# RWKV mixer output computed channel-major from centred values, in a two-layer decoder kernel on one Trainium2 core

## The chip, the cores and the metric

One core of one Trainium2 chip runs the whole program. The metric is the device time of one execution in microseconds (us); the kernel before takes 2488.39 us, the median of three runs. Engine names: PE is TensorE (matmul), PEld its weight load, DVE is VectorE, ACT is ScalarE, POOL is GpSimd, SP is SyncE, which here only issues DMAs.

## The reference, cut to what matters

The program is a decoder trunk of two layers over 256 tokens with model width 2048, in float32. Layer 0 (even) projects the normed input once, and feeds two mixers: differential attention with 8 heads and an RWKV-7 time mix with 16 heads of 64. Layer 1 (odd) is an HGRN2 recurrence. A SwiGLU feed-forward follows each. The change is in the RWKV mixer's output. Of it the reference says:

```python
def step(state, inp):
    rt, wt, kt, vt, kkt, at = inp
    sa = jnp.einsum('bhvk,bhk->bhv', state, -kkt)
    state = state * wt[:, :, None, :] + sa[..., None] * (kkt * at)[:, :, None, :] + vt[..., None] * kt[:, :, None, :]
    return state, jnp.einsum('bhvk,bhk->bhv', state, rt)
...
mean = jnp.mean(y, axis=-1, keepdims=True)
var = jnp.mean(jnp.square(y - mean), axis=-1, keepdims=True)
yn = ((y - mean) * lax.rsqrt(var + RW_GN_EPS)).reshape(B, S, RW_WIDTH) * ln_w + ln_b
bonus = (jnp.sum(r_h * k_h * r_k, axis=-1, keepdims=True) * v_h).reshape(B, S, RW_WIDTH)
return ((yn + bonus) * g).astype(p.dtype)
```

The state, and so y, is linear in the values v. Values from which each head's mean over its 64 channels has been taken give a y that has mean zero in each head.

## The kernel before, in words

Everything is kept channel-major: 128 channels on the partitions, 256 tokens along the free axis. A weight block of 128 output columns is 16 tiles of 128x128. Each block is read from memory by SP, turned into a rounded part on ACT (`Block.high`, line 318) and a remainder on DVE (`Block.low`, line 323), each in two halves of 8 tiles, and multiplied on PE: the rounded part against both parts of the activations (line 333, 512 columns), the remainder against one (line 368, 256 columns). Two converted blocks are resident and two accumulators, `acc`, alternate, so a conversion waits until the block two places before it has been multiplied, and a block's first product waits until DVE has emptied the accumulator (`evacuate`, line 446; in the last step `residual`, lines 1138 and 1140).

The even layer's mixers run in 8 steps, `even_step(j)`, one for each pair of RWKV heads and one attention head. The order in each engine is written out by hand in that function, once for each engine. PE works through the 96 tiles of the next step's six projection blocks, `dense(n)` being the next n tiles, and between them does the small products of the mixers of step j. ACT and DVE put the conversions `high(0..)` and `low(0..)`, numbered by half block, between their mixer work. Each engine runs its own list strictly in the written order. Engines signal through counting semaphores, `S["rw_..."]`. In the last step (`more=False`) the dense tiles are those of the output projection, with all but the two last-made of its 16 input rows.

Two chunks of 128 tokens make an RWKV step. `Vn` are the values turned to token-major, `Us` the solved corrections, `KTR` and `LTR` masked products, `S0` the state between the chunks, `AR` the decayed queries. The output y is token-major in bank 2: for chunk 0 four products with 64 columns (lines 1869 and 1870), for chunk 1 one of 128 (1886) and four of 64 (1889, 1890). The last of them signals `rw_y`. What follows it in the kernel before:

- PE: gate (1894), bonus sums (1896, 1897, signal `rw_bonus`), the 10 dense tiles left, the two transposes of the normalised output (1902, in the trace under the helper's line 1695), which wait for `rw_yn`; then the next step's `rw_za` (1739, 1740), the transposes of its values, the sums of key squares (1747, 1748), 22 dense tiles, and the products `rw_m1` (1757), which wait for `rw_bt`, among others.
- DVE: mean (1364, 1366), subtraction (1368), bonus times value (1372), variance (1374), next values (1151), product with the inverse deviation (1380, `rw_yn`), `evacuate(4)`, `low(13)`, `swap`, `low(14)`; then the next step's scans (1203), and from them a chain to `bk` (1236, `rw_bt`).
- ACT: `key_squares(j + 1)` (737, 738), square of the centred output (855), logarithm (857), exponential (859), a table load, `high(14)`, scale and offset (865), gate copy (867); then the next step's sigmoids (746, 747).

`key_squares` begins with `act.wait_ge(S["rw_bonus"], j)`, called with the next step's number, so with this step's bonus sums: their input `parts` is what it writes over.

Of the kernel before, what the change touches and what calls it, by code (L numbers as in the profile page):

```python
# [13 lines left out]
P = 128  # L14
# [27 lines left out]
C_END = C_QUART + P  # L42
# [4 lines left out]
G_ATT0, G_FFN0, G_ATT1, G_FFN1, G_FIN = 0, 16, 32, 48, 64  # L47
G_LB0, G_LB1 = 80, 96
G_SUB, G_HGN, G_MUW, G_MUG = 112, 113, 114, 115
G_LAM = 116  # L50
# [3 lines left out]
def shape_constants():  # L54
# [18 lines left out]
    c[:, C_QUART:C_QUART + P] = s // 32 == t // 32  # L73
    c[:, C_TRI:C_TRI + P] = s < t
# [15 lines left out]
def build(nc, xT, w_even, w_even_out, w_odd, w_odd_out, w_gu, w_down, w_last, gain_last, consts, gains, par, par_ln, wa_up, g_up, out):  # L90
    with ExitStack() as ctx:
        def sb(name, shape, dt=F32):
            return ctx.enter_context(nc.sbuf_tensor(name, shape, dt))
# [16 lines left out]
        small = sb("small", [P, 96])  # L110
# [17 lines left out]
        def flat(ap):  # L128
            return ap.rearrange("p a b -> p (a b)")
# [32 lines left out]
        yc = take(4, 64)  # L162
        ysq = take(4, 64)
# [80 lines left out]
        ymean = small[:, 20:24]  # L244
        yvar = small[:, 24:28]
        yrs = small[:, 32:36]
# [5 lines left out]
        ars = small[:, 56:58]  # L252
        nrt = small[:, 28:30]
        upper = small[:, 48:52]
        lower = small[:, 92:96]
        hlb = small[:, 60:76]
        homl = small[:, 76:92]
# [4 lines left out]
        def bank(b, n=1):  # L262
            return pm[:, b * 512:(b + n) * 512]
# [9 lines left out]
        for group in (  # L273
# [8 lines left out]
            "rw_S rw_S0 rw_R1 rw_nR1 rw_U1 rw_Us1 rw_y rw_ymean rw_yc rw_ysq rw_yvar rw_yrs rw_yn rw_yT rw_yTs",  # L282
# [383 lines left out]
        def _(act):  # L666
# [73 lines left out]
            def even_step(j, block, more=True):  # L740

                def high(half):
                    block(half // 2).high(act, half % 2)
# [102 lines left out]
                act.activation(Us[:, 0], bank(5)[:, 384:512], ACT.Copy).then_inc(S["rw_Us0"], 1)  # L846
                act.wait_ge(S["rw_R1"], j + 1)
# [3 lines left out]
                high(13)  # L851
                if more:
                    key_squares(j + 1)
                act.wait_ge(S["rw_yc"], j + 1)
                act.activation(ysq, yc, ACT.Square).then_inc(S["rw_ysq"], 1)
                act.wait_ge(S["rw_yvar"], j + 1)
                act.activation(yrs, yvar, ACT.Ln, scale=1.0 / 64, bias=c_gn).then_inc(S["rw_yrs"], 1)
# [4 lines left out]
                act.wait_ge(S["rw_yT"], j + 1)  # L862
                act.wait_ge(S["rw_late"], 32 * j + 32)
                act.wait_ge(S["rw_end"], j + 1)
                act.activation(yT, bank(1)[:, 256:512], ACT.Identity, scale=pln[:, 0:1], bias=pln[:, 1:2]).then_inc(S["rw_yTs"], 1)
# [189 lines left out]
        def _(dve):  # L1055
# [128 lines left out]
            def even_step(j, block, more=True):  # L1184
                def low(half):
                    block(half // 2).low(dve, half % 2)
# [175 lines left out]
                dve.wait_ge(S["rw_y"], j + 1)  # L1362
                y4 = bank(2)[:, 256:512].rearrange("p (a b) -> p a b", a=4)
                dve.reduce_sum(ymean, y4, AX.X).then_inc(S["rw_ymean"], 1)
                dve.wait_ge(S["rw_ymean"], 2 * j + 1)
                dve.tensor_scalar(ymean, ymean, 1.0 / 64, None, ALU.mult).then_inc(S["rw_ymean"], 1)
                dve.wait_ge(S["rw_ymean"], 2 * j + 2)
                dve.tensor_tensor(yc, y4, ymean.unsqueeze(2).broadcast_to([P, 4, 64]), ALU.subtract).then_inc(S["rw_yc"], 1)
# [4 lines left out]
                dve.wait_ge(S["rw_ysq"], j + 1)  # L1373
                dve.reduce_sum(yvar, ysq, AX.X).then_inc(S["rw_yvar"], 1)
# [4 lines left out]
                dve.wait_ge(S["rw_yc"], j + 1)  # L1379
# [302 lines left out]
        def _(pe):  # L1682
# [29 lines left out]
            def even_step(j, block, more=True):  # L1712
# [173 lines left out]
                pe.matmul(bank(2)[:, 384:512], AR[:, 1, 1], S0, start=True, stop=False, skip_group_check=True)  # L1886
                for h in range(2):
                    o, v = bank(2)[:, 384 + 64 * h:448 + 64 * h], slice(64 * h, 64 * h + 64)
                    pe.matmul(o, KTR[:, 2 * h + 1, P:2 * P], Vn[:, 1, v], start=False, stop=False, skip_group_check=True)
                    last = pe.matmul(o, LTR[:, 2 * h + 1, P:2 * P], Us[:, 1, v], start=False, stop=True, skip_group_check=True)  # L1890
                last.then_inc(S["rw_y"], 1)

# [259 lines left out]
```

## Time and profile before

| | |
|---|---|
| time, median of 3 runs (lowest to highest) | 2488.39 us (2487.61 to 2488.83) |
| profiled execution: its own time | 2488.57 us |
| profiled execution: span of the core | 2486.7 us, granted clock 0.999 |
| PE busy | 2468.1 us, 99% |
| DVE, ACT, POOL busy | 1828.9 us (74%), 1236.0 us (50%), 497.9 us (20%) |
| DMA | 438.32 MB, mean 176 GB/s |

The profile is one execution, followed instruction by instruction. Its span is 1.9 us shorter than its own time, which holds some work around the span. A matmul in float32 shows as two records, one in the rounded format or a transpose as one. Ends of matmuls are modelled and overlap the next; the distance between starts is what PE spends. "Idle before" is the time in which an engine had nothing running ahead of an instruction, and behind the arrow stands what ended it.

### The profile page before, as it was taken

What the parts mean: (1) busy time and instruction counts of PE and PEld (TensorE: products, weight loads), DVE (VectorE), ACT (ScalarE), POOL (GpSimd) and SP (SyncE); (2) the same over time, 40 slices, a digit from 0 to 9 for tenths busy, and PEclk for the clock granted to TensorE, in tenths of its full rate; (3) what the DMA queues carried; (4) which work ended last, traced back from release to release, by engine and by line L of the source; (5) the groups of instructions that cost most, each with busy time, mean ns of one, the idle gap of its engine ahead of it and who ended that gap; (6) DMA issues with size and microseconds to landing.
All of it is one profiled execution on the core that took longest, in us unless ns stands there. A gap on an engine that the chain in (4) does not pass through costs nothing.

```text
span 2486.7 us, 45860 instructions
## 1 busy us (share of the span) xinstructions
PE 2468.1 (99%) x16576; PEld 2161.8 (87%) x16576; DVE 1828.9 (74%) x3028; ACT 1236.0 (50%) x1798; POOL 497.9 (20%) x436
## 2 busy tenths in 40 slices
PE   9999999999999999999999999999999999999998
PEld 8888888888888888888888888888888888888887
DVE  7888888766655666566989999997666557655665
ACT  5666666644433443344665656655444434443444
POOL 0123222222200221022222211213222012200220
PEclk9999999999999999999999999999999999999999
DMA  7333233455555555554554445445455555555553
GB/s 273 121 138 133 110 131 120 177 181 192 186 189 192 185 194 186 188 190 173 193 186 169 169 158 179 152 158 216 176 194 186 201 188 186 186 202 185 188 194 127
DMA packets 65570, 438.32 MB, mean 176 GB/s; under 512 B 9408, under 2 KB 10816, under 8 KB 15808
## 3 DMA queue, kind: packets, MB, share of 16 engines
q1 hardware_dynamic: 61632, 436.29, 49.4%
q8 instruction: 64, 1.05, 0.2%
q10 hardware_dynamic: 3840, 0.70, 0.1%
q14 instruction: 34, 0.28, 0.0%
HBM read 434.87 MB, written 2.10 MB: 176 GB/s over the span
## 4 chain that ended last, share of the span: by engine, by line
PE 85%; DVE 8%; issue 4%; ACT 2%; DMA 1%; ACTq 0%; SPq 0%; DVEq 0%
PE acc L333 29%; PE acc L403 17%; PE mixer_banks L414 10%; PE acc L385 9%; PE acc L397 9%; PE acc L368 6%; DVE w_low L323 2%; DVE arena L1568 2%; DVE arena L446 1%; DVE arena L1556 1%; PE mixer_banks L1695 1%; PE acc L330 1%; DVE arena L1558 1%; DMA w_raw<-w_even 1%; PE mixer_banks L1783 0%
## 5 line engine op out<-in xcount | busy, mean ns | idle before, releaser
L318 ACT ACTIVATE w_high<-w_raw 128x1024 fp32r<-128x1024 f32 x831 | 862.9, 1057 | 888.0 <-PE acc L385 387.5
L323 DVE TENSOR_TENSOR w_low<-w_raw,w_high 128x1024 fp32r<-128x1024 f32 x832 | 1047.9, 1286 | 115.3 <-ACT w_high L318 114.4
L333 PE MATMUL acc<-h_split,w_high 128*128 128x512 f32 x3184 | 818.5, 396 | 1.0
L333 PEld LDWEIGHTS acc<-h_split,w_high 128*128 128x128 f32 x3184 | 575.1, 188 | 110.4 <-DVE arena L446 3.1
L565 POOL TENSOR_TENSOR arena<-arena,norm_scale 128x256 f32<-128x256 f32 x152 | 231.3, 1522 | 1348.5 <-DVE arena L446 1328.8
L446 DVE TENSOR_REDUCE arena<-acc 128x256 f32<-128x512 f32 x285 | 196.1, 688 | 289.4 <-PE acc L403 178.2
L403 PE MATMUL acc<-h_split,w_high 128*128 128x512 f32 x1376 | 328.2, 391 | 0.0
L403 PEld LDWEIGHTS acc<-h_split,w_high 128*128 128x128 f32 x1376 | 252.9, 188 | 48.9
L368 PEld LDWEIGHTS acc<-h_split,w_low 128*128 128x128 f32 x1824 | 263.7, 190 | 27.5
L368 PE MATMUL acc<-h_split,w_low 128*128 128x256 f32 x1824 | 273.2, 282 | 0.0
L333 PE MATMUL acc<-mix_split,w_high 128*128 128x512 f32 x752 | 185.6, 392 | 0.6 <-DVE x_residual L1140 0.6
L385 PEld LDWEIGHTS acc<-h_split,w_low 128*128 128x128 f32 x1376 | 176.4, 191 | 6.7
L397 PE MATMUL acc<-h_split,w_low 128*128 128x256 f32 x1376 | 179.1, 283 | 0.0
L385 PE MATMUL acc<-h_split,w_low 128*128 128x256 f32 x1376 | 178.5, 283 | 0.0
L414 PE MATMUL mixer_banks<-w_high,mix_split 128*128 128x512 f32 x704 | 173.9, 389 | 0.0
L397 PEld LDWEIGHTS acc<-h_split,w_low 128*128 128x128 f32 x1376 | 171.3, 192 | 0.0
L333 PEld LDWEIGHTS acc<-mix_split,w_high 128*128 128x128 f32 x752 | 138.1, 188 | 28.1 <-issue 1.3
L414 PEld LDWEIGHTS mixer_banks<-w_high,mix_split 128*128 128x128 f32 x704 | 132.1, 188 | 27.5
L638 POOL TENSOR_TENSOR arena<-arena,norm_scale 128x256 f32<-128x256 f32 x88 | 100.5, 1141 | 47.2 <-ACT arena L943 47.2
L403 PE MATMUL acc<-mix_split,w_high 128*128 128x512 f32 x448 | 107.2, 391 | 0.0
L1138 DVE TENSOR_TENSOR x_residual<-x_residual,acc 128x256 f32 (+1 forms) x80 | 33.5, 419 | 99.2 <-PE acc L403 47.5
L943 ACT ACTIVATE arena<-arena 128x256 f32<-128x256 f32 x88 | 36.9, 419 | 119.5 <-POOL arena L565 119.5
(335 smaller groups left out, 2300.5 us busy)
## 6 DMA issues: line engine op xcount, KB each, us to landing
w_raw<-w_gu SPq DMA_DIRECT2D x176, 1024.0 KB, 4.8
w_raw<-w_odd SPq DMA_DIRECT2D x64, 1024.0 KB, 4.8
w_raw<-w_even SPq DMA_DIRECT2D x49, 1024.0 KB, 4.8
w_raw<-w_last SPq DMA_DIRECT2D x44, 1024.0 KB, 4.8
w_raw<-w_down SPq DMA_DIRECT2D x32, 1024.0 KB, 4.9
w_raw<-w_down SPq DMA_DIRECT2D x16, 768.0 KB, 4.2
w_raw<-w_odd_out SPq DMA_DIRECT2D x12, 1024.0 KB, 4.8
w_raw<-w_even_out SPq DMA_DIRECT2D x10, 1024.0 KB, 4.7
```

Of the source, the lines that this page charges most:

```text
L318: act.activation(wh[:, self.res, ks], raw[:, self.raw, ks], ACT.Copy).then_inc(high_done, 1)
L323: dve.tensor_tensor(wl[:, self.res, ks], raw[:, self.raw, ks], wh[:, self.res, ks].bitcast(F32), ALU.subtract).then_inc(low_done, 1)
L333: pe.matmul(acc[self.acc][:, 0:2 * T], wh[:, self.res, k], flat(both), start=k == 0, stop=stop)
L368: last = pe.matmul(acc[self.acc][:, 0:T], wl[:, self.res, k], split[:, src(k), 0], start=False, stop=k == self.kt - 1, skip_group_check=True)
L385: last = pe.matmul(acc[self.acc][:, 0:T], wl[:, self.res, k], split[:, k, 0], start=False, stop=k == self.kt - 1, skip_group_check=True)
L397: pe.matmul(acc[self.acc][:, 0:T], wl[:, self.res, k], split[:, k, 0], start=k == 0, stop=False, skip_group_check=True)
L403: last = pe.matmul(acc[self.acc][:, 0:2 * T], wh[:, self.res, k], flat(split[:, k]), start=False, stop=k == self.kt - 1, skip_group_check= ...
L414: return pe.matmul(banks[th], split[:, 4 * q + k, c, th * P:(th + 1) * P], flat(w[:, self.res, 4 * k:4 * k + 4]), start=q == 0 and k == 0 ...
L446: dve.reduce_sum(dst, acc[self.acc].rearrange("p (s t) -> p t s", s=2), AX.X).then_inc(evac_done, 1)
L565: pool.tensor_tensor(dst, dst, nrs, ALU.mult).then_inc(S[done], 1)
L638: pool.tensor_tensor(sil[:, b], sil[:, b], nrs, ALU.mult).then_inc(S["hid_scaled"], 1)
L1568: dve.tensor_tensor(*part, ALU.mult).then_inc(S["hg_X"], 1)
```

## The change

In the even steps only:

- The values' transposes become products with a matrix that turns and centres at once: identity less 1/64 within each head. It is a new constant of 128x128, loaded with the others.
- The products for y take their operands the other way round, so that y comes out channel-major: the stationary operand is a head's 64 columns of `Vn` or `Us`, the moving one 128 columns of `KTR` or `LTR`, and the result goes to 64 of the 128 partitions, one head to each half. The mean and its subtraction go away, and so do the two transposes at the step's end.
- The variance is a float32 product of the head ones with the squared output (scaled by 1/8 before the square), in bank 3, and thus there for every channel; the logarithm and exponential are taken of 128x256 in place of 128x4. PE waits for the square ahead of it.
- Four of the ten remaining dense tiles are taken ahead of the gate and bonus products; the variance product stands behind the bonus sums, ahead of the other six.
- `high(13)` on ACT moves ahead of the copies `nR1` and `Us1`; `low(13)` on DVE moves from behind `evacuate(4)` to ahead of the bonus product.
- PE waits for the previous step's `rw_yn` ahead of the sums of key squares, since these write to the bank in which y lies.
- Some small tiles are placed elsewhere, and 16 unused gain columns are left out.

```diff
@@ ACT, even_step
                 act.wait_ge(S["rw_U0"], j + 1)
                 act.activation(Us[:, 0], bank(5)[:, 384:512], ACT.Copy).then_inc(S["rw_Us0"], 1)
+                high(13)
...
                 act.activation(Us[:, 1], bank(2)[:, 0:P], ACT.Copy).then_inc(S["rw_Us1"], 1)
-                high(13)
                 if more:
                     key_squares(j + 1)
-                act.wait_ge(S["rw_yc"], j + 1)
-                act.activation(ysq, yc, ACT.Square).then_inc(S["rw_ysq"], 1)
+                act.wait_ge(S["rw_y"], j + 1)
+                act.activation(ysq, bank(2)[:, 256:512], ACT.Square, scale=1.0 / 8).then_inc(S["rw_ysq"], 1)
                 act.wait_ge(S["rw_yvar"], j + 1)
-                act.activation(yrs, yvar, ACT.Ln, scale=1.0 / 64, bias=c_gn).then_inc(S["rw_yrs"], 1)
+                act.activation(yrs, bank(3)[:, 0:T], ACT.Ln, bias=c_gn).then_inc(S["rw_yrs"], 1)
...
-                act.wait_ge(S["rw_yT"], j + 1)
+                act.wait_ge(S["rw_yn"], j + 1)
...
-                act.activation(yT, bank(1)[:, 256:512], ACT.Identity, scale=pln[:, 0:1], bias=pln[:, 1:2]).then_inc(S["rw_yTs"], 1)
+                act.activation(yT, ysq, ACT.Identity, scale=pln[:, 0:1], bias=pln[:, 1:2]).then_inc(S["rw_yTs"], 1)
@@ DVE, even_step
-                dve.wait_ge(S["rw_y"], j + 1)
-                y4 = bank(2)[:, 256:512].rearrange("p (a b) -> p a b", a=4)
-                dve.reduce_sum(ymean, y4, AX.X).then_inc(S["rw_ymean"], 1)
-                dve.wait_ge(S["rw_ymean"], 2 * j + 1)
-                dve.tensor_scalar(ymean, ymean, 1.0 / 64, None, ALU.mult).then_inc(S["rw_ymean"], 1)
-                dve.wait_ge(S["rw_ymean"], 2 * j + 2)
-                dve.tensor_tensor(yc, y4, ymean.unsqueeze(2).broadcast_to([P, 4, 64]), ALU.subtract).then_inc(S["rw_yc"], 1)
+                low(13)
                 dve.wait_ge(S["rw_bonus"], j + 1)
...
-                dve.wait_ge(S["rw_ysq"], j + 1)
-                dve.reduce_sum(yvar, ysq, AX.X).then_inc(S["rw_yvar"], 1)
...
-                dve.tensor_tensor(yc, yc, yrs.unsqueeze(2).broadcast_to([P, 4, 64]), ALU.mult).then_inc(S["rw_yn"], 1)
+                dve.tensor_tensor(ysq, bank(2)[:, 256:512], yrs, ALU.mult).then_inc(S["rw_yn"], 1)
                 evacuate(4)
-                low(13)
@@ PE, even_step
                 for c in range(2):
-                    last = transposed(bank(4)[:, 256 + c * P:256 + (c + 1) * P], xm[:, 2, c * P:(c + 1) * P])
+                    last = pe.matmul(bank(4)[:, 256 + c * P:256 + (c + 1) * P], xm[:, 2, c * P:(c + 1) * P],
+                                     cst[:, C_CENTRE:C_CENTRE + P], start=True, stop=True)
                 last.then_inc(S["rw_vt"], 1)
+                if not isinstance(j, int) or j > 0:
+                    pe.wait_ge(S["rw_yn"], j)
...
-                for h in range(2):
-                    o, v = bank(2)[:, 256 + 64 * h:320 + 64 * h], slice(64 * h, 64 * h + 64)
-                    pe.matmul(o, KTR[:, 2 * h, P:2 * P], Vn[:, 0, v], start=True, stop=False)
-                    pe.matmul(o, LTR[:, 2 * h, P:2 * P], Us[:, 0, v], start=False, stop=True)
+                for moving, still in ((KTR, Vn), (LTR, Us)):
+                    for h in range(2):
+                        pe.matmul(bank(2)[HALVES[h], 256:384], still[:, 0, HALVES[h]], moving[:, 2 * h, P:2 * P],
+                                  start=still is Vn, stop=still is Us)
...
+                dense(4)
 
                 pe.wait_ge(S["rw_late"], 32 * j + 32)
                 pe.matmul(bank(1)[:, 0:T], gu, sgl, start=True, stop=True).then_inc(S["rw_g"], 1)
                 pe.wait_ge(S["rw_suml"], 2 * j + 2)
                 pe.matmul(bank(0)[:, 0:T], head_r, parts[:, 0], start=True, stop=False)
                 pe.matmul(bank(0)[:, 0:T], head_r, parts[:, 1], start=False, stop=True).then_inc(S["rw_bonus"], 1)
+                pe.wait_ge(S["rw_ysq"], j + 1)
+                pe.matmul(bank(3)[:, 0:T], head_ones, ysq, start=True, stop=True).then_inc(S["rw_yvar"], 1)
                 dense(KT * 6 - done[0])
-                pe.wait_ge(S["rw_yn"], j + 1)
-                for c in range(2):
-
-                    last = transposed(bank(1)[:, 256 + c * P:256 + (c + 1) * P], flat(yc)[:, c * P:(c + 1) * P])
-                last.then_inc(S["rw_yT"], 1)
```

The second chunk's five products are turned in the same way.

## Rows read from the trace of the kernel before

**Rows 1.** The page, busy time of PE over the whole span
```profile
PE 2468.1 (99%) x16576; PEld 2161.8 (87%) x16576; DVE 1828.9 (74%) x3028; ACT 1236.0 (50%) x1798; POOL 497.9 (20%) x436
```
**Rows 2.** Waits of PE, 0 to 700 us: total us, times, longest
```profile
PE mixer_banks L1757 <- issue: 3.2, 6, 0.5
```
**Rows 3.** Timeline of PE, step 2 into 3: start, length, instruction
```profile
193.00 0.52 PE L368 MATMUL acc<-h_split,w_low 128*128 128x256 f32 x3
193.45 0.45 PE L1837 MATMUL mixer_banks<-arena 64*64 64x64 f32 x8
193.82 0.66 PE L1842 MATMUL mixer_banks<-arena 128*128 128x64 f32 x4
...
198.58 0.39 PE L1866 MATMUL mixer_banks<-arena 128*128 128x128 f32 x2
198.80 0.33 PE L1869 MATMUL mixer_banks<-arena 128*128 128x64 f32 x2
...
199.62 0.71 PE L333 MATMUL acc<-h_split,w_high 128*128 128x512 f32 x2
...
203.99 0.65 PE L1894 MATMUL mixer_banks<-arena 128*128 128x256 f32 x2
...
204.59 0.28 PE L1897 MATMUL mixer_banks<-head_sum_parts,head_ones_r 128*128 128x256 f32 x1
204.71 0.62 PE L333 MATMUL acc<-h_split,w_high 128*128 128x512 f32 x2
...
205.41 2.00 PE L333 MATMUL acc<-h_split,w_high 128*128 128x512 f32 x8
...
209.15 0.44 PE L1695 MATMUL mixer_banks<-constants_sb,arena 128*128 128x128 f32 x2
209.34 0.36 PE L1747 MATMUL mixer_banks<-head_sum_parts,head_ones_r 128*128 128x256 f32 x1
...
216.63 0.87 PE L368 MATMUL acc<-h_split,w_low 128*128 128x256 f32 x6
218.04 1.14 PE L1757 MATMUL mixer_banks<-arena 64*128 64x256 f32 x8 [0.53 <-issue]
```
**Rows 4.** Timeline of ACT, the same stretch
```profile
204.97 0.51 ACT L737 ACTIVATE head_sum_parts<-arena 128x256 fp32r<-128x256 f32 x1 [1.38 <-PE mixer_banks L1897]
205.39 0.49 ACT L738 ACTIVATE arena<-arena 128x256 f32<-128x256 f32 x1
205.79 0.40 ACT L855 ACTIVATE arena<-arena 128x256 f32<-128x256 f32 x1
...
207.00 0.21 ACT L859 ACTIVATE small<-small 128x4 f32<-128x4 f32 x1
207.23 1.28 ACT L860 ACT_TABLE_LOAD   x1
208.52 1.06 ACT L318 ACTIVATE w_high<-w_raw 128x1024 fp32r<-128x1024 f32 x1
...
214.36 0.40 ACT L761 ACTIVATE arena<-arena 128x256 f32<-128x256 f32 x1
214.79 0.51 ACT L763 ACTIVATE arena<-arena,small 128x256 f32<-128x256 f32 x1
```
**Rows 5.** Timeline of DVE, the same stretch
```profile
209.67 1.41 DVE L323 TENSOR_TENSOR w_low<-w_raw,w_high 128x1024 fp32r<-128x1024 f32 x1
211.00 1.77 DVE L1203 TENSOR_TENSOR_SCAN arena<-constants_sb,arena 128x128 f32<-128x128 f32 x2
...
217.51 0.42 DVE L1236 TENSOR_TENSOR arena<-arena 128x256 f32<-128x256 f32 x1
```
**Rows 6.** Timeline of DVE, last even step
```profile
456.75 0.42 DVE L1140 TENSOR_TENSOR x_residual<-x_residual,acc 128x256 f32<-128x256 f32 x1
```
**Rows 7.** Timeline of PE, last even step
```profile
453.17 0.65 PE L1894 MATMUL mixer_banks<-arena 128*128 128x256 f32 x2
...
457.32 2.08 PE L333 MATMUL acc<-mix_split,w_high 128*128 128x512 f32 x8 [0.26 <-DVE x_residual L1140]
```

More of the change, by code:

```diff
@@ L41 @@
 C_QUART = C_IDQ + 32
-C_END = C_QUART + P
+C_CENTRE = C_QUART + P
+C_END = C_CENTRE + P
 P_MU, P_W0, P_A0, P_KK, P_KA, P_RK = 0, 3, 4, 5, 6, 7
 NPAR = 8
[L47 to L50, printed above, removed]
+G_ATT0, G_FFN0, G_ATT1, G_FFN1 = 0, 16, 32, 48
+G_LB0, G_LB1 = 64, 80
+G_SUB, G_HGN, G_MUW, G_MUG = 96, 97, 98, 99
+G_LAM = 100
 NG = G_LAM + 256
@@ L73, in shape_constants @@
     c[:, C_QUART:C_QUART + P] = s // 32 == t // 32
+    c[:, C_CENTRE:C_CENTRE + P] = np.eye(P) - (s // 64 == t // 64) / 64.0
     c[:, C_TRI:C_TRI + P] = s < t
@@ L109, in build @@
         gn = sb("gains_sb", [P, NG])
-        small = sb("small", [P, 96])
+        small = sb("small", [P, 88])
         x = sb("x_residual", [P, KT, T])[:]
@@ L161, in build @@
         S0 = take(P)
-        yc = take(4, 64)
-        ysq = take(4, 64)
+        yrs = take(T)
+        ysq = take(T)
         rn = take(T)
@@ L243, in build @@
         scl = small[:, 18:19]
-        ymean = small[:, 20:24]
-        yvar = small[:, 24:28]
-        yrs = small[:, 32:36]
         amx = small[:, 36:40]
@@ L251, in build @@
         aln = small[:, 54:56]
-        ars = small[:, 56:58]
+        ars = small[:, 32:34]
         nrt = small[:, 28:30]
         upper = small[:, 48:52]
-        lower = small[:, 92:96]
-        hlb = small[:, 60:76]
-        homl = small[:, 76:92]
+        lower = small[:, 20:24]
+        hlb = small[:, 56:72]
+        homl = small[:, 72:88]
         acc = [ctx.enter_context(nc.psum_tensor(f"acc{i}", [P, 512], F32)) for i in range(2)]
@@ L281, in build @@
             "rw_m1 rw_m2 rw_LTR rw_L rw_KTR rw_T0 rw_TT rw_TQ rw_Tf rw_T5 rw_X rw_N rw_Z rw_Zs rw_TXT rw_kbT rw_kbn rw_R0 rw_nR0 rw_U0 rw_Us0",
-            "rw_S rw_S0 rw_R1 rw_nR1 rw_U1 rw_Us1 rw_y rw_ymean rw_yc rw_ysq rw_yvar rw_yrs rw_yn rw_yT rw_yTs",
+            "rw_S rw_S0 rw_R1 rw_nR1 rw_U1 rw_Us1 rw_y rw_ysq rw_yvar rw_yrs rw_yn rw_yTs",
             "rw_g rw_gs rw_rounded rw_out rw_end rw_scaled",
@@ L1378, in even_step @@
                 dve.wait_ge(S["rw_yrs"], 2 * j + 2)
-                dve.wait_ge(S["rw_yc"], j + 1)
-                dve.tensor_tensor(yc, yc, yrs.unsqueeze(2).broadcast_to([P, 4, 64]), ALU.mult).then_inc(S["rw_yn"], 1)
+                dve.tensor_tensor(ysq, bank(2)[:, 256:512], yrs, ALU.mult).then_inc(S["rw_yn"], 1)
                 evacuate(4)
-                low(13)
                 if more:
@@ L1885, in even_step @@
                 pe.wait_ge(S["rw_Us1"], j + 1)
[L1886 to L1890, printed above, removed]
+                pe.matmul(bank(2)[:, 384:512], S0, AR[:, 1, 1], start=True, stop=False, skip_group_check=True)
+                for moving, still in ((KTR, Vn), (LTR, Us)):
+                    for h in range(2):
+                        last = pe.matmul(bank(2)[HALVES[h], 384:512], still[:, 1, HALVES[h]], moving[:, 2 * h + 1, P:2 * P],
+                                         start=False, stop=still is Us, skip_group_check=True)
                 last.then_inc(S["rw_y"], 1)
+                dense(4)
                 pe.wait_ge(S["rw_late"], 32 * j + 32)
@@ L2128 @@
     for at, v in ((G_ATT0, attn_norm_g[0]), (G_FFN0, ffn_norm_g[0]), (G_ATT1, attn_norm_g[1]), (G_FFN1, ffn_norm_g[1]),
-                  (G_FIN, final_norm_g), (G_LB0, hg_lower_bound[0]), (G_LB1, hg_lower_bound[1]), (G_SUB, da_subln_g[0]),
+                  (G_LB0, hg_lower_bound[0]), (G_LB1, hg_lower_bound[1]), (G_SUB, da_subln_g[0]),
                   (G_HGN, hg_norm_g[0]), (G_MUW, mu[3072:3200])):
```

## The prediction

> **What bounds the kernel now.** I read the busy times first: PE is busy 99% of the span, no other engine over 74% [rows 1]. So a change costs or gives what PE's own list gets longer or shorter, plus what PE has to wait. I then read PE's waits over the even layer. In the stretch that the diff touches there is one that repeats: six times 0.53 us ahead of line 1757 [rows 2, 3]. Its real size is a bit more. The six products ahead of it start at 216.63 and take 0.12 us each, so PE is done at about 217.35 and starts again at 218.04.
>
> What ends this wait comes from the three timelines of one transition, step 2 into 3. DVE's product 1236 ends at 217.93 [rows 5] and PE starts 0.11 us behind it. Back from there DVE works through one chain without a gap that matters, down to the scans at 211.00, which stand behind `low(14)` at 209.67 [rows 5]. That conversion waits for `high(14)` on ACT, which runs from 208.52 to 209.58 behind a table load, which stands behind the exponential that ends at 207.21 [rows 4]. So the length of a transition is set by a chain: y done, inverse deviation, table load, `high(14)`, `low(14)`, scans, `bk`, line 1757. The end of the exponential is its handle: later by so much, the step is longer by so much. PE's own list comes about 0.55 us earlier and is hidden.
>
> **The change part by part**, in one transition, on that chain.
>
> *From y to the exponential before.* PE leaves y at 203.99 (start of 1894), the exponential ends at 207.21: 3.22 us [rows 3, 4]. In between ACT does the two key squares, which begin only behind the bonus sums [rows 4].
>
> *After: dense(4).* Two tiles take 0.70 us (204.71 to 205.41) [rows 3], four 1.40 us. They only change place for PE, but bonus sums, and all behind them, come 1.40 us later than y.
>
> *Gate and bonus*: unchanged, 203.99 to 204.71, 0.72 us [rows 3].
>
> *The new wait.* PE's list now says: bonus sums, wait for `rw_ysq`, variance product. ACT's list says: key squares, then the square. And the key squares wait for these same bonus sums. So PE sends the bonus sums and stands still until ACT has done all three. ACT starts 0.38 us after the start of 1897 (204.59 to 204.97); the two key squares take 0.82 us (204.97 to 205.79), the square 0.40 us, from PSUM about the same [rows 3, 4]; 0.10 us for the signal, as at line 1757. That is 1.70 us from the start of 1897, of which 0.12 us is that product itself: PE idles 1.58 us. Nothing covers it, since six dense tiles stand behind the waiting product and PE keeps its order. Line 1757 shows the same: PE stands there until its signal comes [rows 3].
>
> *Variance product.* 128 columns in float32 take two records at 0.11 us (198.58 to 198.80 for one product) [rows 3]. 256 columns are then twice that, 0.43 us for PE. The logarithm can start when the last record has drained: about 0.62 us after the start, from the 0.65 us modelled for 1894, which has this shape.
>
> *Logarithm and exponential* on 256 columns in place of 4: 0.43 us from the start of one to that of a dependent one, then 0.51 us (761 and 763) [rows 4]: 0.94 us. The table load then follows as before.
>
> Sum from y to the exponential: 1.40 + 0.72 + 1.58 + 0.62 + 0.94 = 5.26 us, against 3.22: **2.04 us later**.
>
> *What DVE saves* (two reductions, the scaling and the subtraction, some 1.4 us) lies between y and the exponential, or beside ACT's work, and is off the chain. The same holds for `low(13)`, taken out from between `evacuate(4)` and `swap`: before, DVE is ready for `low(14)` at 209.67, and `high(14)` ends at 209.58. DVE will be ready 1.2 us sooner and wait for ACT. That move is worth 0.1 us at most. `high(13)` in its new place fills an idle stretch of ACT and costs nothing, while its half block is free by then.
>
> *The products for y.* Each group of four is now 0.82 us (198.80 to 199.62) [rows 3]: eight records at 0.11, bound by the weight load, since 64 columns would need less. After, each has 128 columns, 0.11 us per record of pure streaming, so eight in a row are 0.88 us and nothing is won, unless the two heads' products run side by side in the two halves of the array. The nearest row is 1837, 64x64 products that alternate between halves of the output: eight records from 193.45 to 193.82. One at a time they need 0.055 us each, 0.44 in all. They take 0.37, and that with the change back to the full array; the three tiles ahead of them (0.12 each from 193.00) were over at 193.35, so 0.10 us went into the change of tiling, and as much, I assume, into the way back. That leaves 0.27 us for eight, four pairs side by side at 0.06. I take this: four pairs at 0.11 and 0.20 for two changes, 0.64 us, so -0.2 us for each group, **-0.4 us** for a step. The bounds: side by side with no cost of changing -0.4 a group; one after another with two changes, 1.08 us, +0.25 a group.
>
> The Trainium skill (TensorEngine Tiling, sections Performance Considerations and Key Properties) says that swapping stationary and moving operand with two column tiles gives up to 2x, and that a change of tiling mode drains the engine. By the first alone a group would be 0.41 us, and the result some 3 us lower than the forecast; on the second the rows agree, with 0.10 us.
>
> *The centring product.* The values' two transposes take 0.19 us (209.15 to 209.34) [rows 3], two float32 products of this size 0.44: +0.25 us on PE. The step's last two transposes, -0.2 us. Both stand behind the chain's fork, on PE's hidden list only. This list changes by 1.58 + 0.43 + 0.25 - 0.2 - 0.4 = +1.66 us against the chain's +1.64, so the wait at 1757 stays about 0.5 us. In step 0 there was no wait at 1757, and there the 0.25 us counts. PE's new wait for `rw_yn` ahead of 1747 costs nothing: that product ends about 0.5 us behind the exponential, and 1747 comes at least 2 us behind it (209.34 against 207.21, both shifted alike) [rows 3, 4]. What it costs if the exponential slips by more than that: the rest, one to one.
>
> *The last step* has no key squares, so no stall there. PE leaves y at 453.17, DVE's `residual(4)` ends 4.00 us later, at 457.17, and PE waits for it at 457.32 [rows 6, 7]. After, the exponential is over 1.40 + 0.72 + 0.62 + 0.94 = 3.68 us after y, and three DVE products follow, the normalising one and the two of `residual`, at 0.42 us (1140) [rows 6] or a little less since they overlap: 4.9 us. That is +0.9, less 0.4: +0.5 us. The gated output of this step is late too, but has 5 us of products to hide behind.
>
> *The start.* 64 KB more of constants, behind which two weight blocks are queued; DMA is not what PE waits for by then: 0 to 0.3 us, I take 0.1.
>
> **Total:** 7 transitions x (2.04 - 0.40) = 11.5; last step 0.5; step 0 0.25; start 0.1; and I round up for the weight load that the variance product can't have ahead of its wait, 0.1 in seven: 13.0 us. The profiled execution's own time is 2488.57 us (1.9 over its span), within 0.2 us of the median: **2501.5 us**.
>
> **Rivals.** *A: no pairs.* The halves run one after another: +0.25 for a group in place of -0.2, so +0.9 us in each of 8 steps, 7.2 us: 2508.5 us. For it: moving operands here have all 128 rows, those of 1837 only 64, and no row of before has two such at once. Against it: the pairing in 1837 itself is between output halves.
>
> *B: not slower.* The place is the gap between the bonus sums and the variance product. If ACT had the square ready there (the key squares not held by the bonus sums), the stall would go: 7 x (2.04 - 1.58 - 0.40) + 0.5 + 0.25 + 0.1 = 1.3 us, 2489.8, no change to be measured. It decides when the stall is under some 0.5 us: 7 x (0.06 + 0.5) + 0.85 = 4.8 us. Against it: `key_squares` waits for this step's sums by its count, and the profile shows ACT idle 1.38 us until exactly them [rows 4]. To be faster it would need the products for y at their best too, 3 us less.
>
> *C: more slips.* The new chain pushes the following step's conversions, or the output of the last step, into another wait, or PE's idle time brings the granted clock down for a while. Half a microsecond in each step is 4 us on the forecast, a whole one 8: 2505 to 2510. Against it: conversions for blocks ahead keep their distance, since all shift alike, and the clock is 0.999 over a run with a wait of similar length.
>
> **How the numbers follow.** Chances: forecast 0.57 (its own range 2497 to 2505), A 0.20, C 0.14, B 0.09, of which 0.03 is a gain. A measurement of this kernel can tell about 0.2%, 5 us, from no change. Slower by over that: 0.57 + 0.20 + 0.14 = 0.91; same 0.06; faster 0.03. The range leaves out B and the far end of C: low from the best case of the products (13.0 - 3.2 = 9.8, less 3 for the small terms), 2495; high from A, 2509.
>
> **What the profile after would show.** Right: PE idle some 1.6 us ahead of the variance product in seven steps, released by ACT's square; ACT's order bonus, 737, 738, square, without a gap; transitions 1.6 to 1.8 us longer; the wait at 1757 still near 0.5 us; each group for y at about 0.65 us; DVE waiting for `high(14)`. Wrong: the variance product following the bonus sums at once (B); groups of 1.1 us (A); a wait of PE that was not there, ahead of 1747 or the first dense tile of a step (C).

## The result and the profile after

The changed kernel takes 2499.45 us (median of 5 runs, 2499.1 to 2500.49) beside 2488.74 us for the kernel before (5 runs): 10.7 us slower, a ratio of 1.0042 with a 95% interval of 1.0031 to 1.0052. The forecast was 13.0 us, 2501.5 us, with a range of 2495 to 2509.

The profiled execution spans 2497.7 us (before 2486.7), at a granted clock of 0.999 as before. PE is busy 2472.4 us, 4.3 us more, so the other 6.7 of the 11.0 us are PE standing still. PE's waits over the even layer, 0 to 700 us of the changed kernel, in us in total, times, and the longest:

```profile
PE mixer_banks L1892 <- ACT arena L854: 9.3, 7, 1.3
PE mixer_banks L1690 <- DVE small L1071: 3.6, 1, 3.6
PE mixer_banks L1749 <- DVE arena L1231: 1.8, 1, 1.8
PE acc L332 <- DVE x_residual L1139: 0.9, 1, 0.9
PE mixer_banks L1857 <- ACT arena L845: 0.4, 1, 0.4
```

Line numbers have moved: 1892 is the variance product, 854 the square of y, 1749 what was 1757, 317 and 322 the conversions. The seven waits ahead of 1892 are new. The six of 0.53 us ahead of 1757 [rows 2] are gone from the list. What is left at 1749 is the one of the transition into the last step, 1.8 us, which the kernel before has as well:

```profile
PE mixer_banks L1757 <- DVE arena L1232: 1.8, 1, 1.8
PE acc L333 <- DVE x_residual L1140: 0.3, 1, 0.3
```

The timeline of PE in the changed kernel, step 2 into 3, which answers to [rows 3]:

```profile
201.69 0.39 PE L1858 MATMUL mixer_banks<-arena 128*128 128x128 f32 x2
202.01 0.66 PE L1861 MATMUL mixer_banks<-arena 128*64 128x128 f32 x8
202.60 0.73 PE L332 MATMUL acc<-h_split,w_high 128*128 128x512 f32 x2
...
206.84 0.72 PE L332 MATMUL acc<-h_split,w_high 128*128 128x512 f32 x2
...
208.88 0.28 PE L1890 MATMUL mixer_banks<-head_sum_parts,head_ones_r 128*128 128x256 f32 x1
210.49 0.70 PE L1892 MATMUL mixer_banks<-arena,constants_sb 128*128 128x256 f32 x2 [1.33 <-ACT arena L854]
...
213.85 0.71 PE L1732 MATMUL mixer_banks<-constants_sb,arena 128*128 128x128 f32 x4
214.32 0.36 PE L1739 MATMUL mixer_banks<-head_sum_parts,head_ones_r 128*128 128x256 f32 x1
...
221.59 0.87 PE L367 MATMUL acc<-h_split,w_low 128*128 128x256 f32 x6
222.39 1.15 PE L1749 MATMUL mixer_banks<-arena 64*128 64x256 f32 x8
```

And ACT and then DVE in the same stretch, which answer to [rows 4, 5]:

```profile
209.26 0.51 ACT L736 ACTIVATE head_sum_parts<-arena 128x256 fp32r<-128x256 f32 x1 [3.62 <-PE mixer_banks L1890]
209.67 0.49 ACT L737 ACTIVATE arena<-arena 128x256 f32<-128x256 f32 x1
210.07 0.36 ACT L854 ACTIVATE arena<-mixer_banks 128x256 f32<-128x256 f32 x1
211.23 0.47 ACT L856 ACTIVATE arena<-mixer_banks,small 128x256 f32<-128x256 f32 x1 [0.79 <-PE mixer_banks L1892]
211.73 0.42 ACT L858 ACTIVATE arena<-arena 128x256 f32<-128x256 f32 x1
```
```profile
214.55 1.23 DVE L322 TENSOR_TENSOR w_low<-w_raw,w_high 128x1024 fp32r<-128x1024 f32 x1 [0.86 <-ACT w_high L317]
215.71 1.27 DVE L1202 TENSOR_TENSOR_SCAN arena<-constants_sb,arena 128x128 f32<-128x128 f32 x2
...
221.75 0.42 DVE L1235 TENSOR_TENSOR arena<-arena 128x256 f32<-128x256 f32 x1
```

Three things are to be read from these rows. First, the circle. PE issues the bonus sums at 208.88; ACT, idle for 3.62 us, is released by them at 209.26, does two key squares and the square of y, and lets PE go on at 210.49. PE was free at 209.00 (0.12 us for that product), so it stands for 1.49 us, and this repeats seven times. The wait has a small price on top: the two records of 1892 start 0.32 us apart here and 0.21 us in square_first (below), where nothing is waited for. Here the weight load of 1892 starts only with the product, at 210.49; there it starts 0.11 us ahead of it. Second, from the end of the exponential (212.15) to the end of DVE's last product on the chain (222.17) it is 10.02 us; before, from 207.21 to 217.93, it was 10.72 [rows 4, 5]. That chain has become 0.7 us shorter, which was not forecast. `low(14)` and the two scans take 1.23 and 1.27 us in place of 1.41 and 1.77. Third, because of that, PE goes from its dense tiles (221.59, six at 0.12, and 0.1 for the change of tiling) straight into 1749. It is close: DVE's product was over 0.22 us before 1749 started, where the signal needs some 0.11 us.

So the distance from one 1757 or 1749 to the next is 51.42 us in place of about 50.15, +1.27, where +1.64 was forecast. By the starts of these products: step 0 comes 0.59 us later (67.54 to 68.13), the seven transitions take 9.44 us more together, and from there to the first product of the last block in step 7 it is 0.64 us more (38.06 to 38.70 us). That is 10.7 of the 11.0 us between the two spans. The 0.59 us of step 0 are not safe: the same stretch, with the same instructions, ends anywhere from 67.51 to 68.24 us in the profiles of the changed kernel and its variants below.

### The profile page after: what moved, and what is told of

It reads as the page before. It is cut to its first block, busy times and chain, and to the rows that moved or that the text cites. A ratio compares the mean times of both kernels' runs of the same rounds, so it can differ in the third digit from the quotient of the medians.

```text
span 2497.7 us, 45852 instructions
## 1 busy us (share of the span) xinstructions
PE 2472.4 (99%) x16592; PEld 2159.8 (86%) x16592; DVE 1816.8 (73%) x2996; ACT 1239.5 (50%) x1798; POOL 492.5 (20%) x436
## 4 chain that ended last, share of the span: by engine, by line
PE 86%; DVE 7%; issue 4%; ACT 2%; DMA 0%; SPq 0%; ACTq 0%; DVEq 0%
PE acc L332 29%; PE acc L402 17%; PE mixer_banks L413 9%; PE acc L384 9%; PE acc L396 9%; PE acc L367 6%; DVE w_low L322 2%; DVE arena L1557 1%; DVE arena L445 1%; DVE arena L1545 1%; PE acc L329 1%; DVE arena L1547 1%; PE mixer_banks L1684 1%; PE mixer_banks L1775 0%; DMA w_raw<-w_even 0%
```

## The experiments

Each was timed in 5 rounds (5 to 11 executions) beside the kernel before on the same chip; of the last there is one execution. Chips differ between the groups of rows, so a small difference between two kernels is better taken from their ratios. "Transition" is the distance between the first m1 products (line 1749 or 1757) of steps 2 and 3 in its own profile.

| kernel | us | before, beside it | ratio, 95% interval | transition |
|---|---|---|---|---|
| the change | 2499.45 | 2488.74 | 1.0042 (1.0031 to 1.0052) | 51.42 |
| square_first | 2491.66 | 2489.43 | 1.0006 (0.9997 to 1.0015) | 50.10 |
| no_hoist | 2497.08 | 2489.43 | 1.0030 (1.0018 to 1.0041) | 51.41 |
| conv_back | 2504.41 | 2489.43 | 1.0060 (1.0047 to 1.0074) | 51.95 |
| before_conv | 2485.80 | 2489.43 | 0.9985 (0.9976 to 0.9994) | 49.59 |
| square_first_no_hoist | 2485.99 | 2488.77 | 0.9987 (0.9978 to 0.9996) | 49.84 |
| dense_between | 2488.19 | 2488.77 | 0.9997 (0.9988 to 1.0006) | 49.82 |
| unpaired | 2499.66 | 2488.77 | 1.0041 (1.0027 to 1.0055) | 51.42 |
| before_conv_product | 2486.83 | 2488.77 | 0.9991 (0.9982 to 1.0000) | 49.87 |
| short_chain_conv_back | 2486.42 | 2489.08 | 0.9988 (0.9979 to 0.9997) | 49.84 |
| halves_apart | 2507.18 (one run) | 2489.08 | - | 52.20 |

### The order on ACT

```diff
+                act.wait_ge(S["rw_y"], j + 1)
+                act.activation(ysq, bank(2)[:, 256:512], ACT.Square, scale=1.0 / 8).then_inc(S["rw_ysq"], 1)
                 if more:
                     key_squares(j + 1)
-                act.wait_ge(S["rw_y"], j + 1)
-                act.activation(ysq, bank(2)[:, 256:512], ACT.Square, scale=1.0 / 8).then_inc(S["rw_ysq"], 1)
```

> The changed kernel with one swap on ACT: the square of y ahead of the next step's key squares. Order theory (PE idles because its variance product waits for a square that stands behind key squares, which wait for PE's bonus sums): PE's idle time ahead of the variance product, 1.3 us in each of 7 steps, goes. The chain to the exponential gets shorter by less, since the key squares (0.8 us) now stand between the variance product and the logarithm: the exponential ends 1.1 us sooner after y. So 7 x 1.1 = 7.7 us less, 2491.5 to 2492.5 us. Rival (the added work makes it slower: variance product, wider logarithm and exponential, float32 centring): no change beyond 1 us, 2499.5.

2491.66 us, as the order theory had it. The variance product follows the bonus sums at once, and on ACT the logarithm (856) now stands behind the key squares. PE, then ACT, in square_first:

```profile
205.94 0.28 PE L1890 MATMUL mixer_banks<-head_sum_parts,head_ones_r 128*128 128x256 f32 x1
206.06 0.59 PE L1892 MATMUL mixer_banks<-arena,constants_sb 128*128 128x256 f32 x2
...
218.16 0.49 PE L1749 MATMUL mixer_banks<-arena 64*128 64x256 f32 x2 [0.24 <-issue]
```
```profile
204.01 0.39 ACT L852 ACTIVATE arena<-mixer_banks 128x256 f32<-128x256 f32 x1 [1.31 <-PE mixer_banks L1881]
206.32 0.51 ACT L736 ACTIVATE head_sum_parts<-arena 128x256 fp32r<-128x256 f32 x1 [1.92 <-PE mixer_banks L1890]
206.73 0.49 ACT L737 ACTIVATE arena<-arena 128x256 f32<-128x256 f32 x1
207.13 0.45 ACT L856 ACTIVATE arena<-mixer_banks,small 128x256 f32<-128x256 f32 x1
```

Two lines exchanged on ACT take back 7.8 of the 10.7 us. A transition is 1.32 us shorter, of the 1.58 (1.49 and the slower start) that the wait cost. The rest turns into the small wait at 1749, since the chain became shorter by less than PE's list did. The square is done at 204.4, long before it is wanted; its place behind the key squares was all that made PE wait.

By the trace, the seven transitions together are 9.1 us shorter, more than the 7.8 of the times. What comes between is TensorE's clock in the last step. There PE waits 2.21 us at 1749, and behind it the same products take twice as long as in the changed kernel, where the wait is 1.77 us. First the changed kernel's rows, then those of square_first, and the granted clock (`PEclk`, third number from the end) in stretches of square_first:

```profile
429.29 1.14 PE L1749 MATMUL mixer_banks<-arena 64*128 64x256 f32 x8 [1.77 <-DVE arena L1231]
430.23 1.14 PE L1755 MATMUL mixer_banks<-arena 64*128 64x256 f32 x8
```
```profile
419.85 2.09 PE L1749 MATMUL mixer_banks<-arena 64*128 64x256 f32 x8 [2.21 <-DVE arena L1231]
421.69 1.79 PE L1755 MATMUL mixer_banks<-arena 64*128 64x256 f32 x8
```
```profile
416.00:419.80 3.80, 1.65 (x11) 1.26 (x9) 3.70 (x8) 3.22 (x6) 1.34 (x2) 0.98 0.04 5
419.80:421.70 1.90, 1.85 (x9) 1.64 (x11) 1.87 (x4) 0.55 (x1) 0.00 (x0) 0.50 0.00 0
423.50:425.00 1.50, 1.50 (x13) 1.08 (x11) 1.22 (x3) 1.04 (x4) 0.31 (x1) 1.00 0.83 349
```

The clock is at 0.50, that is 1.2 in place of 2.4 GHz, from 419.65 to 423.06 us; PE stood still before it fell and was busy when it rose. From 1749 to the next dense tile it takes 4.24 us in place of 2.66, 1.6 us more. The eleven executions of square_first lie in two groups that fit this: five from 2489.9 to 2490.3 us, and six, with the profiled one, from 2491.7 to 2492.5 us at a mean clock lower by 0.001. The median is from the upper group; without the fall the exchange is worth about 9.4 us. Why the clock falls in some executions and not in others isn't shown.

### What sets a transition: PE's list or the chain

```diff
                 last.then_inc(S["rw_y"], 1)
-                dense(4)
```

> The changed kernel without the four dense tiles ahead of the gate and bonus products (they stay behind the variance product). Theory 1, PE's own list with the idle stretch in it sets the transitions: the idle stretch has the same length wherever the bonus sums stand, so the seven transitions keep 51.4 us; only the last step, where PE waits 0.95 us for an evacuation behind the exponential, gains: 2498.6 us. Theory 2, as in the prediction, the chain over the exponential sets them: it is 1.4 us shorter, 7 x 1.4 = 9.8 and 0.9, 2489 us.

Here the gate and bonus products come right behind y, the standing still with them, and the exponential ends 1.4 us sooner after y (3.92 us in place of 5.31). The transition stays 51.41 us. That speaks for theory 1: after the change, PE's own list with its hole sets the length, and a sooner exponential is worth nothing in these transitions. The total is 2.4 us less, where 0.9 was expected. Beside the wait in the last step (0.9 us gone), the transition into the last step falls from 52.61 to 51.26 us, which the expectation overlooked: there the chain over the exponential is what is waited for, 1.8 us at 1749, before and after the change.

### The two conversions

```diff
                 act.activation(Us[:, 0], bank(5)[:, 384:512], ACT.Copy).then_inc(S["rw_Us0"], 1)
-                high(13)
...
                 act.activation(Us[:, 1], bank(2)[:, 0:P], ACT.Copy).then_inc(S["rw_Us1"], 1)
+                high(13)
...
-                low(13)
                 dve.wait_ge(S["rw_bonus"], j + 1)
...
                 evacuate(4)
+                low(13)
```

> The changed kernel with high(13) and low(13) in their old places. Overlap theory (low(13) at its old place runs beside POOL's rotation products and slows both, and what they push along slows low(14) and the scans): the chain from the exponential to line 1757 is 0.6 us longer again, PE's list hides 0.1 of it: 7 x 0.5 = 3.5 us more, 2503. The prediction's figure (worth 0.1 us at most): 2499.5 to 2500.

The same move in the other direction, made in the kernel before and nothing else:

```diff
+                low(13)
                 dve.wait_ge(S["rw_y"], j + 1)
                 y4 = bank(2)[:, 256:512].rearrange("p (a b) -> p a b", a=4)
...
                 evacuate(4)
-                low(13)
```

and `high(13)` on ACT as in the change.

> The kernel before with nothing but the two conversions sooner: high(13) ahead of the copies nR1 and Us1, low(13) ahead of the mean of y. Overlap theory: the chain behind the exponential is 0.6 us shorter, and line 1757, which waits 0.55 to 0.6 us for it, comes 0.5 us sooner: 7 x 0.5 = 3.5 us less, 2485. The prediction's figure: at most 0.1 us in a step, 2488 to 2488.7.

conv_back takes 5.0 us more than the change, before_conv 3.6 us less than before. The transitions say the same in both: this move alone is worth 0.5 us (51.95 against 51.42; 49.59 against 50.15). In conv_back the six waits ahead of 1749 are back, 0.5 us each, and in before_conv those ahead of 1757 are gone. The transition into the last step gains nothing by the move (52.61 and 52.60; 50.88 against 50.75), so the seven together are 3.2 and 3.3 us. The 5.0 us are more than that: three of the five executions of conv_back have the lower mean clock, as six of square_first have, and the profiled one, with no fall of the clock in the even layer, took 2502.67 us, 3.2 us more than the change. What the move does is seen on POOL and DVE. In conv_back, POOL, then DVE:

```profile
214.31 1.65 POOL L597 TENSOR_TENSOR arena<-arena,constants_sb 128x256 f32<-128x256 f32 x1 [2.33 <-DVE arena L445]
215.92 1.72 POOL L599 TENSOR_TENSOR arena<-arena,constants_sb 128x256 f32<-128x256 f32 x1
217.72 0.74 POOL L602 TENSOR_TENSOR arena<-arena 128x256 f32<-128x256 f32 x1
```
```profile
214.15 1.22 DVE L322 TENSOR_TENSOR w_low<-w_raw,w_high 128x1024 fp32r<-128x1024 f32 x1
...
215.29 0.45 DVE L1146 STREAM_SHUFFLE arena<-arena 128x256 f32<-128x256 f32 x1
215.62 1.41 DVE L322 TENSOR_TENSOR w_low<-w_raw,w_high 128x1024 fp32r<-128x1024 f32 x1
216.96 1.77 DVE L1202 TENSOR_TENSOR_SCAN arena<-constants_sb,arena 128x128 f32<-128x128 f32 x2
```

And the same three products of POOL in the changed kernel, with `low(13)` gone from there:

```profile
213.29 0.73 POOL L597 TENSOR_TENSOR arena<-arena,constants_sb 128x256 f32<-128x256 f32 x1 [2.34 <-DVE arena L445]
213.97 0.73 POOL L599 TENSOR_TENSOR arena<-arena,constants_sb 128x256 f32<-128x256 f32 x1
214.78 1.60 POOL L602 TENSOR_TENSOR arena<-arena 128x256 f32<-128x256 f32 x1
```

POOL's products start behind `evacuate(4)` in both. With `low(13)` beside it, the first takes 1.65 us in place of 0.73 and is still running when `low(14)` starts; the second takes 1.72 us and runs into the first scan, the third lies beside the second scan. `low(14)` takes 1.41 in place of 1.23 us, and the two scans 1.77 in place of 1.27. In the changed kernel POOL isn't out of the way either: its third product falls onto `low(14)` and the first scan. But it starts 0.23 us after `low(14)`, and then it is POOL that gets longer (1.60 us) and not the conversion (1.23). What is won on the chain is the second scan, which has POOL no longer beside it: taken one by one, the scans are 0.95 and 0.90 us in conv_back, 0.96 and 0.40 us in the changed kernel. Two engines that slow each other make a chain longer that neither is late on by its own list. That they slow each other is what these rows show; by which resource, no run here shows.

### A version with neither fault

Three kernels have the square first and no dense tiles ahead of the bonus sums. square_first_no_hoist is just that. dense_between puts the four tiles between the bonus sums and the variance product. short_chain_conv_back is the first of these with the two conversions in their old places.

> The changed kernel with the square ahead of the key squares and without the four dense tiles ahead of the bonus sums. No idle stretch, and the exponential is over some 2.8 us after y (in square_first 4.2), so PE's own list alone sets the transitions: 51.42 less 1.49 us of standing still, 49.9 us each (before with the conversions sooner: 49.6), the last one 1.4 us shorter than in square_first, and the 0.95 us wait in the last step gone. 2487 to 2488 us: below the kernel before, and still 1.3 us above before with the conversions sooner. If the added products cost nothing on PE's list, 2485 to 2486.

> As square_first_no_hoist, but the four dense tiles stand between the bonus sums and the variance product. PE's list has the same length, and its variance product is never waited for. The exponential is over 3.7 us after y, 0.9 us later than in square_first_no_hoist. If PE's list sets the six middle transitions: 49.9 us each as there; only the transition into the last step and the last step itself (0.9 us each) are longer: 1.8 us more than that kernel, 2489 us. If the chain sets them all: 0.9 x 7 and 0.9, 7 us more.

> square_first_no_hoist with high(13) and low(13) in their old places. Its chain over the exponential is some 2.5 us shorter than in the changed kernel, so 0.5 us more on it is hidden behind PE's own list: middle transitions stay at 49.84 us, only the one into the last step may grow by up to 0.6; 2486 to 2486.7 us. If the conversions' place has a price of its own wherever they stand (0.53 us in each transition, as from the changed kernel to conv_back): 2489.7.

All three have the same middle transition, 49.82 to 49.84 us, with the exponential over 2.76 us after y in two of them and 3.73 in the third, and with the conversions in either place: PE's list alone sets it. In short_chain_conv_back the move that was worth 0.5 us a transition in the change is worth nothing (2486.42 against 2485.99 us, in intervals that overlap). dense_between loses its 2 us where it was expected, in the transition into the last step (51.06 against 50.05 us) and in the last step. square_first_no_hoist is 2.8 us faster than before; before_conv, 3.6 us. Those two differ from each other by less than their intervals. Both beat both kernels.

The 49.84 us against 49.59 in before_conv is the price of the new arithmetic when nothing waits: 0.25 us a step. By the traces: centring products 0.28 and variance product 0.43 more; the last transposes 0.2 and the two groups for y 0.13 each less; +0.25. Nothing is left over for the small tiles placed elsewhere and the gain columns left out, which were not tried by themselves.

### The centring product by itself

```diff
-                    last = transposed(bank(4)[:, 256 + c * P:256 + (c + 1) * P], xm[:, 2, c * P:(c + 1) * P])
+                    last = pe.matmul(bank(4)[:, 256 + c * P:256 + (c + 1) * P], xm[:, 2, c * P:(c + 1) * P], ident,
+                                     start=True, stop=True)
```

This is before_conv with one more edit; the identity turns and doesn't centre, so the arithmetic stays that of before.

> Before with the conversions sooner, where PE's list sets the transitions, and the values turned by a float32 product with the identity in place of two transposes: the centring product's price by itself. By the traces 0.47 us for two products against 0.19 for two transposes: 0.28 us in each of 8 steps, 2.2 us over before_conv (2485.8): 2488. If it were hidden, as in the kernel before, no change: 2485.8.

The transition grows from 49.59 to 49.87 us, the 0.28 that the traces gave for it. The times say less: 1.0 us more, or 1.7 if each is taken against its own runs of before, against 2.2 expected, and both are within the intervals.

### Are the two heads' products side by side?

> The changed kernel with the four products of each group for y in the order head 0, head 0, head 1, head 1 in place of alternating heads. Pairing theory (two heads' products run side by side in the two halves of the array): a group takes 0.88 us and 0.2 for the changes of tiling in place of 0.69, 0.4 us more, 16 groups, 6 us: 2505 to 2506 us. Rival (they run one after another anyway, and are fast because the weight load is of 64 columns only): no change, 2499.5.

```diff
-                for moving, still in ((KTR, Vn), (LTR, Us)):
-                    for h in range(2):
+                for h in range(2):
+                    for moving, still in ((KTR, Vn), (LTR, Us)):
```

No change, 2499.66 us. The pairing theory had been given a consequence that it need not have: by the starts of the records, here too they come in pairs, 0.01 us apart, 0.10 to 0.15 us from pair to pair, as in the change. So PE must have taken the other head's products alongside though they stood behind in its list; the trace doesn't name the half of a record. So a second look, with other work between the halves, in chunk 0's group only:

```diff
                 for h in range(2):
                     for moving, still in ((KTR, Vn), (LTR, Us)):
                         pe.matmul(bank(2)[HALVES[h], 256:384], still[:, 0, HALVES[h]], moving[:, 2 * h, P:2 * P],
                                   start=still is Vn, stop=still is Us)
-                dense(2)
+                    if h == 0:
+                        dense(2)
```

> The changed kernel with the two dense tiles behind chunk 0's group for y moved between the two products of head 0 and the two of head 1, so that no two products of different halves are neighbours. Pairing theory: the four records of one head follow each other at 0.11 us, so the group takes 0.88 us of streaming in place of 0.44, and 0.2 for two more changes of tiling: transitions 0.6 us longer, 52.0 us. Rival (a product for 64 outputs takes half the time by itself): records at 0.055 us, 0.2 us longer, 51.6 us.

PE in halves_apart:

```profile
203.06 0.65 PE L1861 MATMUL mixer_banks<-arena 128*64 128x128 f32 x4
203.65 0.72 PE L332 MATMUL acc<-h_split,w_high 128*128 128x512 f32 x2
204.21 0.40 PE L367 MATMUL acc<-h_split,w_low 128*128 128x256 f32 x2
204.53 0.65 PE L1861 MATMUL mixer_banks<-arena 128*64 128x128 f32 x4
205.12 0.49 PE L1867 MATMUL mixer_banks<-arena 128*128 128x128 f32 x2
```

Four records of one head take 0.59 us, from 203.06 to 203.65. In the change, eight records of both heads take the same 0.59, from 202.01 to 202.60. So the two halves do run side by side, and the pairing theory holds; rival A is out. The transition is 52.20 us, 0.78 more: 0.59 for four records in a stretch of their own with the way back to the full array, 0.09 for the change into the tiling, and 0.10 at 1867, whose two records now start 0.21 us apart in place of 0.11. Of the 7.7 us over the change, 1.6 are again the clock: it is at 0.50 from 434.52 to 437.93 us, from just behind the wait of 1.77 us at 1749 in the last step.

## Why the prediction was right, point by point

**The new wait** was the forecast's main term and is what happened: 1.58 us forecast, 1.49 measured, seven times, in the place and with the releaser named. The 0.1 us that the forecast added for the weight load is there too, 0.11 us between the two records; the transition without the wait is 49.84 us, so the wait costs 1.58 us in all. square_first shows that the order on ACT is its cause: without it, and with all the new arithmetic, 2491.66 us.

**From y to the exponential**: 5.26 us forecast, 5.31 measured (206.84 to 212.15). The sum is closer than its terms, which is luck: the dense tiles took 1.49 us (1.40 forecast), gate and bonus 0.67 (0.72), the wait 1.49 (1.58), and from the start of the variance product to the logarithm it was 0.74 (0.62).

**The conversions: the mis-sized term.** "That move is worth 0.1 us at most" failed. It was sized by asking when DVE would be ready for `low(14)`, with each instruction's length taken as fixed. It measured 0.7 us on the chain and 0.5 in a transition. That `low(14)` starts sooner is indeed worth 0.06 us (2.46 us behind the exponential before, 2.40 after); the rest is that `low(14)` and the second scan became shorter, as POOL's products fell elsewhere. The rows for it stood in the trace of before: `low(14)` at 1.41 us and the scans at 1.77 [rows 5] are longer than the same instructions elsewhere in that trace (most of the conversions take 1.22 us; the second scan takes 0.39 us in step 0 and 0.90 in the next six), and were not asked why.

**What sets a transition.** Because of that term "the wait at 1757 stays about 0.5 us" was wrong too. The chain is now done sooner than PE's list, so the list sets the length. PE's list of before without its wait is 49.59 us, by before_conv, and of the change 51.42: +1.83, where +1.66 was forecast (the groups for y won 0.26 and not 0.4 us). Less 0.56 us of wait that was there before gives +1.27 in place of +1.64, and so the transitions are not "1.6 to 1.8 us longer", as the prediction's list of signs has it. Six times the difference is 2.2 us. The transition into the last step, where the chain still rules and the conversions' place is worth nothing, was +1.86, 0.2 over the forecast. The seven together are 9.44 us, against 11.5 and 0.7 for the weight load.

**The products for y**: right in kind, 0.69 us a group with the changes of tiling (201.91 to 202.60) against 0.64 forecast and 0.82 before. The factor of two that the Trainium skill (TensorEngine Tiling, Performance Considerations) gives for two column tiles is reached inside the group: 0.59 us for both halves, and 0.59 for one half alone in halves_apart. For the whole group against before it is not, 0.69 us for 0.82: four pairs at 0.11 are 0.44 us, and the other 0.25 goes with the two changes of tiling. The forecast's own way, from the rows of 1837, was the closer one.

**The centring product**: 0.28 us against 0.25. It is hidden or not as PE's list is: in the kernel before, the 0.53 us wait would have covered it (this was not run), and where PE's list rules it is paid in full.

**The last step**: 0.64 us against 0.5, with the wait for the evacuation at 0.95 us. **Step 0 and the start**: 0.59 us against 0.35, which shows little, as the same stretch differs by 0.7 us between profiles of like kernels; whether the larger constants cost anything isn't shown.

**Rivals.** B, not slower, was against the rows and did not happen; square_first shows that its price was right: without the stall a transition is 50.10 us beside 50.15 before, where B had +0.06, and the kernel is within 0.2% of before. For A, 0.44 us in each of 16 groups is 7.0 us; the 7.2 comes of rounding on the way, while the 2508.5 goes with 7.0. Of C, no new wait came up in the changed kernel, and its profile shows no fall of the clock in the even layer. But the fall that C names is real, as square_first and halves_apart show, at 1.6 us a time; one of the changed kernel's five executions, the one of 2500.49 us, has the lower mean clock.

## What to carry to other kernels

When an edit makes an engine wait for a result of another, read the other engine's list from that result backwards: if something ahead of it waits for the first engine, the wait costs a round trip however early the data was there. Here, exchanging two lines on an engine that is not the bottleneck took back most of the loss, while the arithmetic that the change saved lay on DVE and ACT, off what PE waited for. An instruction that is longer than its like elsewhere in the trace can have another engine beside it, as here, and moving a third one can take the two apart; but it counts only while the chain they are on is what the bottleneck waits for. And where the times of two edits and their traces disagree, as here 7.8 and 9.1 us, look at the granted clock behind the long waits before trusting the median.

## What the runs showed of the hardware

Products for different halves of the output (64 columns of the array each, 128 rows) ran side by side although the list had both of one head first: pairs 0.01 us apart, in the same 0.59 us. A change to that tiling cost 0.09 us, and 0.78 us a transition went into splitting one group in two.

DVE and POOL products in float32, falling onto each other, got longer: POOL's on 128x256 from 0.73 to between 1.60 and 1.72 us, a DVE scan of 128x128 from 0.40 to between 0.90 and 0.96 us, a DVE conversion of 128x1024 from 1.22 to 1.41 us. Of a conversion and a POOL product it was the one that started second that got longer: a conversion that was already running when POOL's product started kept its 1.22 or 1.23 us. For the scans that doesn't hold throughout: a POOL product that started 0.2 us before the end of the first scan in conv_back kept its 0.74 us.

TensorE's clock fell from 1.00 to 0.50 for 3.41 us, at the end of a wait of 2.21 us in one profile and just behind one of 1.77 us in another, and cost about 1.6 us each time; in the changed kernel's profile it stayed at 1.00 behind the same wait of 1.77 us.
